# Filling the gaps of a sequential recurrence: projections in halves of four products instead of quarters of two

## The reference, cut to what matters

```
def rwkv_scan(S0, r, w, kk, kka, kt, v):
    def step(S, inp):
        r_t, w_t, kk_t, kka_t, k_t, v_t = inp
        sk = jnp.einsum('bhvk,bhk->bhv', S, kk_t)
        S = S * w_t[:, :, None, :] - sk[..., None] * kka_t[:, :, None, :] + v_t[..., None] * k_t[:, :, None, :]
        return S, jnp.einsum('bhvk,bhk->bhv', S, r_t)
    ...
```

## Time and profile before

| what | value |
|---|---|
| median of 3 runs | 4537.6 us (4534.05 to 4546.19) |
| profiled execution | 4534.05 us, span 4531.9 us |
| TensorE busy over the span | 3915.0 us (86%) |
| VectorE, ScalarE busy | 1662.6 us (37%), 971.0 us (21%) |
| mean granted TensorE clock | 0.927 of full speed |
| the 20 chunks of the first layer | 709.37 to 1274.00 us |
| the 20 chunks of the second layer | 2962.20 to 3530.00 us |

### The profile page before, as it was taken

How to read it: one execution, slowest core, us unless ns; L and a number is a source line. 1 busy time by engine, 2 the same in 40 slices (tenths; PEclk the granted TensorE clock), 3 DMA queues, 4 the chain that set the end, 5 groups by cost and what they waited for, 6 DMA issues and landing times. The chain is left out here.

```text
span 4531.9 us, 81404 instructions
## 1 busy us (share of the span) xinstructions
PE 3915.0 (86%) x34256; PEld 2607.9 (58%) x34256; DVE 1662.6 (37%) x3896; ACT 971.0 (21%) x2266; POOL 223.7 (5%) x226
## 2 busy tenths in 40 slices
PE   5886779999879978999968777799998799699998
PEld 3674446777778843444346644467777787334443
DVE  1445535555532232111124545455555322311111
ACT  2221223333321110000022212233333211100000
POOL 0001100000000000111100011000000000011110
PEclk8998889999989978999979989799999899799999
DMA  5400000000022137999853010000000221389997
GB/s 209 175 6 34 17 31 19 19 17 3 3 100 71 68 162 272 399 393 397 313 211 139 4 34 32 18 17 19 18 3 3 105 70 63 162 309 394 394 398 301
DMA packets 86965, 612.23 MB, mean 135 GB/s; under 512 B 14132, under 2 KB 26420, under 8 KB 52292
## 3 DMA queue, kind: packets, MB, share of 16 engines
q1 hardware_dynamic: 74308, 583.88, 32.8%
q0 software_dynamic: 12288, 23.07, 2.3%
HBM read 581.19 MB, written 30.97 MB: 135 GB/s over the span
## 5 line engine op out<-in xcount | busy, mean ns | idle before, releaser
L2510 PE MATMUL ps<-expert_w,expert_xT 128*64 128x512 f32 x2048 | 459.0, 601 | 3.2 <-DVE expert_xT L2599 3.2
L2510 PEld LDWEIGHTS ps<-expert_w,expert_xT 128*64 128x64 f32 x2048 | 142.6, 138 | 289.0 <-issue 285.3
L1269 PE MATMUL ps<-merge_h_high,merge_w_high 128*128 128x320 f32 x768 | 261.1, 340 | 19.6 <-DVE merge_h_low L1333 19.6
L973 PE MATMUL ps<-w_da,hT 128*128 128x384 f32 x640 | 236.2, 520 | 40.8 <-DVE da_stat L1114 30.7
L1270 PE MATMUL ps<-merge_h_low,merge_w_high 128*128 128x320 f32 x768 | 238.9, 311 | 0.0
L1271 PE MATMUL ps<-merge_h_high,merge_w_low 128*128 128x320 f32 x768 | 238.7, 311 | 0.0
L2515 PE MATMUL ps<-expert_w,expert_xT 128*32 128x256 f32 x4096 | 234.3, 380 | 0.0
L2510 PE MATMUL ps<-expert_w,expert_hT_l 128*64 128x512 f32 x1024 | 226.8, 595 | 0.5 <-ACT expert_hT_l L2584 0.5
L1276 PE MATMUL ps<-yT,merge_w 128*128 128x320 f32 x768 | 222.1, 432 | 0.0
L1587 PE MATMUL ps<-hT,w_rw 128*128 128x320 f32 x640 | 212.2, 459 | 0.6
L2515 PEld LDWEIGHTS ps<-expert_w,expert_xT 128*32 128x32 f32 x4096 | 126.5, 110 | 129.0 <-issue 52.1
(11 more groups left out here) (424 smaller groups left out, 7108.4 us busy)
## 6 DMA issues: line engine op xcount, KB each, us to landing
expert_w<-in_w_expert SPq DMA_DIRECT2D x192, 2048.0 KB, 18.2
w_mod_ring<-in_w_mod SPq DMA_DIRECT2D x32, 1024.0 KB, 7.3
merge_w<-in_w_merge SPq DMA_DIRECT2D x48, 512.0 KB, 3.7
w_mod_first<-in_w_mod SPq DMA_DIRECT2D x8, 2048.0 KB, 14.6
w_ml<-in_w_ml SPq DMA_DIRECT2D x6, 2048.0 KB, 7.8
w_da<-in_w_da SPq DMA_DIRECT2D x8, 1536.0 KB, 6.6
w_rw<-in_w_rw SPq DMA_DIRECT2D x8, 1536.0 KB, 6.4
merge_w<-in_w_merge SPq DMA_DIRECT2D x48, 256.0 KB, 3.9
```

Source lines behind the costliest of these rows:

```text
L973: m = nc.tensor.matmul(g.ps[:, bank_of(h, t), 0:3 * P], g.hT[:, k, tile(t)], w[:, k, :], start=k == 0, stop=k == KB - 1)
L1269: nc.tensor.matmul(bank, high[:, k], xh, start=q == 0 and k == 0, stop=False)
L2510: m = mm(g.ps[64 * n:64 * n + 64, bank, :], lhs, w[:, j, kk, 512 * n:512 * n + 512], start=first, stop=last)
```

## The change

`project` issues nothing at its even quarters, and at each odd one four products instead of two. Per head that has a next one, twelve gaps become empty and twelve others hold four products (eight records). The last product of a projection stays in the gap in which it was, with the signal to ScalarE; the wait for the bank and for the weights moves one gap later.

```diff
                 def project(h, i, q):
+                    if q % 2 == 0:
+                        return
                     which, p = {K: (1, 0), K + 1: (1, 1), R: (0, 0), R + 1: (0, 1), V: (2, 0), V + 1: (2, 1)}[i]
                     bank = g.ps[:, 7 * (i % 2), 0:HALF]
-                    if q == 0:
+                    if q == 1:
                         side(h, i)
                         if i == K:
                             arrived = pe.snap(l * (16 * (H + 1)) + 16 * (h + 3))
                             pe.wait_ge(g.w_rw_loaded, arrived)
-                    for k in (2 * q, 2 * q + 1):
+                    for k in range(2 * q - 2, 2 * q + 2):
                         m = mm(bank, w[:, k, which, :], g.hT[:, k, half(p)], start=k == 0, stop=k == KB - 1)
                     if q == 3:
                         m.then_inc(side_ready[i % 2], 1)
```

## The result

| | before | after |
|---|---|---|
| median | 4541.9 us (4 runs, 4534.05 to 4552.18) | 4587.19 us (4 runs, 4583.2 to 4589.38) |
| ratio, 95% interval | | 1.010 [1.0076, 1.0124] |
| profiled span | 4531.9 us | 4585.7 us |
| mean granted TensorE clock | 0.927 | 0.919 |
| first layer's loop to the start of the last chunk | 540.19 us | 566.07 us |

The kernel got 45 us slower. The forecast, 4557 in a range of 4545 to 4570, was 19 us above the median that it started from and 15 above the one in the table. Of the 53.8 us between the two spans, 48.8 lie in the two loops over the chunks. Another 4.2 had passed before the first chunk began (713.58 against 709.37). In all the other profiles taken here it began between 711.0 and 713.6, so there the kernel before had an early one, and the change has no part in it.

A forecast was written before the change was run, and what follows sets the result against it. TensorE's own list sets the pace in most places, VectorE's in a few stretches. Per head 12.03 us less 9.28 gives 2.75, in all 16.5; added to 4537.6 with 3 us for the clock: 4557, range 4545 to 4570.

The forecast's parts named there:

- the sum for the order: All gaps: doubled ones cost 12.03 us per head, emptied ones return 9.28, so 2.75 more per head, 16.5 in all.
- Quarter prices by gap: Emptied gaps: a quarter returns 1.14 us in gaps 0 and 2, 0.77 in gap 7, 1.27 in gap 5 of chunk 0.
- 1.08 us for four more records: Doubled gaps: ten of twelve per head each take 1.08 us more, 10.8 us together.
- nothing back from gap 5 of chunks 1 and 3: Emptied gap 5 there returns nothing, as VectorE times the stretch; 1.22 us of waiting becomes 2.5 in chunk 1.
- The choice in gap 3 (slack by starts, 0.63): Doubled gap 3, chunks 2 and 4: 0.45 us of slack leaves a cost of 0.63; shown idle time would leave 0.90.
- The clock term: Gap 5 of chunks 1 and 3: 12 new waits bring 4 falls to half clock, 6 us, counted half as 3.
- The rate: From chunk 4: 2 of 6 waits for VectorE with gap 5 empty have a clock drop, applied to 12 new waits.
- The price: From chunk 4, 29.74 us in head 0 against 28.22 in head 1: one clock drop costs 1.52 us.
- the clock drops at each bare wait: Rival: all twelve new waits without filler lose the clock at 1.52 us each, 18 us on top, 4572; chance 0.10.
- The even swap: Rival: each moved quarter costs what it returns, -4 us in all, 4533; chance 0.24, including a loss under 13.6 us.
- the release of gap 5: Rival: in chunks 1 and 3 the wait goes with its quarter, 26 us less, 4528; chance 0.06.
- no effect: Rival: nothing changes since ScalarE and VectorE get each projection at the same place; ruled out beforehand, no chance given.

The follow-up runs named there:

- experiment 1: The changed kernel with R and V, the projections that begin in gap 5 of chunks 1 and 3, back in quarters: 4551.89 us, ratio 1.0025 to the kernel before.
- the halves with covers: The changed kernel plus throwaway products in gap 5 of chunks 1, 3 and 4 and gap 8 of chunk 2: 4539.56 us, ratio 0.9997.
- the quarters with covers: The kernel before plus throwaway products, two in gap 8 of chunk 2 and three in gap 5 of chunk 4: 4527.0 us, ratio 0.9967.

## Why the prediction was wrong

*The direction and the sum for the order were right.* Quarter prices by gap, 1.08 us for four more records, nothing back from gap 5 of chunks 1 and 3, 0.45 us of slack in gap 3: each term stands in the chunk times at full clock, 2.83 us per head for 2.75. Only in chunk 0 of head 0 did gap 3 return 0.6, not nothing, 1.2 us in all. The choice in gap 3 (slack by starts, 0.63) is borne out, as L1677 now starts 0.92 us after L1740; 0.90 by the idle time shown would have been off.

*The clock term failed.* It was the step "At the same rate that is 4 drops, 6 us ... so I count half: 3 us". Measured, the two loops of the changed kernel hold 1132.15 - 2 x 542.05 = 48 us of lost clock, those of the kernel before 1083.35 - 2 x 534.2 = 15 us, so the change cost 33 us there, where the forecast had 3. Both factors were too low. The sign that I had named for being wrong, mean clocks under 1.00 in chunks 1 and 3 of more than half the heads, is there in all six.
- The rate. I took it from chunk 4, whose wait idles 2.02 us. The one that the change makes in chunk 1 idles 2.49 (2.69 in head 0). Over all profiles here, chunk 1 with a bare gap 5 had a drop in 23 of 24 heads, and with anything in the gap (idle 1.42 or less) in 0 of 48. The other new wait, the 1.93 us in chunk 3, had none in the changed kernel and 11 in the 30 heads where it is bare.
- The price. A drop in the rows of before cost 1.52 us. In the changed kernel chunk 1 lost 3.1 (34.45 - 31.37), and what starts at the end of chunk 2 lost 0.6 there and 3.8 in chunk 3 (34.96 - 31.18). The doubled gap 6, partly at half clock, alone took 0.96 us more.
- The place. I looked for drops at the waits that the change makes. More than half the loss, 4.4 of 7.5 us per head, starts at the old wait in gap 8 of chunk 2. Counting waits one by one can't foresee that.

The rival "the clock drops at each bare wait" named the right mechanism and had 0.10. Its count was not right: of the twelve new waits six were followed by a drop, those in chunk 1. Its 4572 also had the same too small price. Its argument against, that head 1 has the same wait without a drop, was a sample of six. The uncovered chunk 4 shows over eight kernels with that gap bare how little six say: 2, 0, 6, 4, 2, 6, 3 and 4 heads of six had a drop there, with one and the same wait of 2.0 us.

*The even swap, the release of gap 5 and no effect* are out: a half costs its 1.08, L1740 stays 11.03 us behind the first copy.

The same pattern in all heads of the changed kernel goes with one length: each stretch at half clock follows the same one a head earlier by 157.0 us, a whole number of steps of the grid, so that every head meets the grid at the same places. What stays open is why the drops settle there and spread differently in other kernels. No run here predicts a pattern from a list of waits.

The Trainium skill (TensorE: Matmul & The Clock Gate, "HAM oscillation — how this bites in real kernels") describes a kernel whose clock falls again in every wait between two bursts of matmuls, and advises to arrange the work so that TensorE stays warm. These traces agree on the mechanism, but the waits of its example are longer than any here: drops followed waits of 1.37 to 2.69 us. Covering them was worth 47 us to the changed kernel, while its order of the work costs 16.

## What to carry to other kernels

Work placed in a wait pays twice: for its own time, and for the clock of what follows. Before moving filler out of a wait, price the loss at half clock of everything behind it. Here the longest bare wait lost the clock in 23 of 24 heads, and waits of 1.9 to 2.0 us in 38 of 78. Length is not the whole of it: the 1.37 us in gap 8 of chunk 2 was followed by a drop in 32 of 42 heads, the 1.42 us in chunk 1 of head 0 in none of 12. To compare two orders, cover the long waits in both with throwaway matmuls; then the chunk times of heads 1 and 2 follow the sum to 0.1 us, and the covers may be worth keeping.

## What the runs showed of the hardware

- Throwaway f32 matmuls of 128x320 ahead of four waits per head made the changed kernel 47.6 us faster, and ahead of two the one before 13 us, though they add work to the bound engine.
- The same wait at the same place was followed by a drop or by none. The 48 bare waits of 2.0 us in chunk 4 sort without an exception by where their end falls between two points at which the granted clock can change.
- Half clock can last though TensorE has work: PE is busy 10.20 of the 10.20 us at 0.50 in the window from 960.50 above.
- Runs of one kernel spread by 15 us in ten runs of experiment 1, by 7 in ten of the halves with covers and by 3.5 in seven of the quarters with covers.
